# VectorE, not GpSimd, makes the low parts of the weight slabs by default

## Time and profile before

| | us |
|---|---|
| median of three runs | 2493.86 |
| time of the profiled execution | 2493.3 |
| its span, first to last instruction | 2491.5 |
| TensorE busy | 2474.3 |
| VectorE / ScalarE / GpSimd busy | 1116.7 / 1036.4 / 1133.0 |

### The profile page before, as it was taken

How to read it: one execution, slowest core, us unless ns; L and a number is a source line. 1 busy time by engine, 2 the same in 40 slices (tenths; PEclk the granted TensorE clock), 3 DMA queues, 4 the chain that set the end, 5 groups by cost and what they waited for, 6 DMA issues and landing times.

```text
span 2491.5 us, 32310 instructions
## 1 busy us (share of the span) xinstructions
PE 2474.3 (99%) x12882; PEld 2119.1 (85%) x12882; DVE 1116.7 (45%) x2339; ACT 1036.4 (42%) x2012; POOL 1133.0 (45%) x651
## 2 busy tenths in 40 slices
PE   9999999999999999999999999999999999999998
PEld 8888898888889888889888888888898888888887
DVE  7682486755415632325144545423232446434313
ACT  7552487742335322235343333333343443333323
POOL 3354355544445554444434445444544435444442
PEclk9999999999999999999999999999999999999999
DMA  5233332245332553322322222223322222222232
GB/s 213 76 102 103 94 84 75 64 161 192 138 128 85 191 198 112 104 93 77 118 76 85 85 81 88 86 86 100 110 93 85 85 77 81 89 89 81 93 97 81
DMA packets 89237, 258.79 MB, mean 104 GB/s; under 512 B 8961, under 2 KB 30209, under 8 KB 88705
## 3 DMA queue, kind: packets, MB, share of 16 engines
q1 hardware_dynamic: 89088, 256.74, 30.8%
HBM read 246.22 MB, written 2.10 MB: 100 GB/s over the span
## 4 chain that ended last, share of the span: by engine, by line
PE 91%; DVE 4%; ACT 3%; issue 1%; POOL 0%; DMA 0%; DVEq 0%; SPq 0%; POOLq 0%; ACTq 0%
PE bank L1829 89%; PE bank L1839 2%; ACT PP L2047 1%; DVE pt_lo L2350 0%; DVE Y L2350 0%; DVE nt L2350 0%; DVE C L2350 0%; DVE PP L2609 0%; ACT pt_hi L2047 0%; ACT Hhi L2047 0%; ACT blkv L2047 0%; ACT blkk L2047 0%; ACT w_hi L2047 0%; DMA XR<-in_x 0%; POOL n L2915 0%
## 5 line engine op out<-in xcount | busy, mean ns | idle before, releaser
L2910 POOL TENSOR_TENSOR w_lo<-w_raw,w_hi 128x1024 fp32r<-128x1024 f32 (+1 forms) x302 | 747.3, 2477 | 877.6 <-ACT w_hi L2047 877.4
L1829 PE MATMUL bank<-Hhi,w_hi 128*128 128x512 f32 (+1 forms) x1636 | 634.1, 388 | 0.0
L1829 PE MATMUL bank<-Hlo,w_hi 128*128 128x512 f32 (+1 forms) x1636 | 626.9, 383 | 0.1
L1829 PE MATMUL bank<-Hhi,w_lo 128*128 128x512 f32 (+1 forms) x1636 | 626.8, 383 | 0.0
L2047 ACT ACTIVATE w_hi<-w_raw 128x1024 fp32r<-128x1024 f32 (+1 forms) x318 | 326.2, 1030 | 139.2 <-DMA w_raw<-in_wa 82.5
L1829 PEld LDWEIGHTS bank<-Hhi,w_lo 128*128 128x128 f32 x1636 | 307.7, 188 | 61.5
L1829 PEld LDWEIGHTS bank<-Hlo,w_hi 128*128 128x128 f32 x1636 | 308.5, 189 | 53.4 <-POOL w_lo L2910 0.5
L1829 PEld LDWEIGHTS bank<-Hhi,w_hi 128*128 128x128 f32 x1636 | 308.2, 188 | 52.8
L2910 POOL TENSOR_TENSOR w_fifth_lo<-w_fifth_raw,w_fifth_hi 128x1024 fp32r<-128x1024 f32 x77 | 189.9, 2467 | 216.3 <-ACT w_fifth_hi L2047 216.3
L1829 PE MATMUL bank<-Hhi,w_fifth_hi 128*128 128x512 f32 x404 | 159.6, 395 | 0.0
L1829 PE MATMUL bank<-Hhi,w_fifth_lo 128*128 128x512 f32 x404 | 157.8, 390 | 0.0
(11 more groups left out here) (411 smaller groups left out, 4687.6 us busy)
## 6 DMA issues: line engine op xcount, KB each, us to landing
w_raw<-in_wb SPq DMA_DIRECT2D x169, 512.0 KB, 3.3
w_raw<-in_wa SPq DMA_DIRECT2D x139, 512.0 KB, 3.4
wm<-in_w_ada SPq DMA_DIRECT2D x48, 512.0 KB, 4.5
w_fifth_raw<-in_wb SPq DMA_DIRECT2D x42, 512.0 KB, 3.3
w_fifth_raw<-in_wa SPq DMA_DIRECT2D x35, 512.0 KB, 3.4
QQ<-Y SPq DMA_DIRECT2D x64, 128.0 KB, 2.4
wa_raw<-in_wb SPq DMA_DIRECT2D x5, 512.0 KB, 6.1
XR<-in_x SPq DMA_DIRECT2D x4, 512.0 KB, 7.6
```

The costliest lines, as they stand in the source:

```text
L1829: return self.e.matmul(o, lhs, rhs, start=start, stop=stop)
L2910: self.e.tensor_tensor(x.lo[:, k:k + n, :], x.raw[:, k:k + n, :], f(x.hi[:, k:k + n, :]), ALU.subtract).then_inc(*w_rest(s, k))
```

## The change

The default engine of cut_to changes from "pool" to "dve". Calls that name an engine are as before, and so are the order of the walk, the slots, the DMAs and the roundings.

```
-        def cut_to(self, s, n=8, by="pool"):
+        def cut_to(self, s, n=8, by="dve"):
             while self.cut <= s and self.cut < self.sent:
                 for k in range(0, 8, n):
                     self.round_weights(self.cut, self.slot[self.cut], k, n)
                     self.rest_weights(self.cut, self.slot[self.cut], k, n, by)
                 self.parts[self.cut], self.rested[self.cut] = n, dve_rest if by == "dve" else w_rest
```

## The result

The changed kernel takes 2542.39 us (median of 4 runs, 2538.97 to 2544.28) against 2493.89 for the kernel before (2493.67 to 2494.07): a ratio of 1.0192, 95% interval 1.018 to 1.0205. It is 48.5 us slower. The forecast was 2500.2, its range ended at 2509. The profiled execution took 2541.4 us with a span of 2539.6, 48.1 more than the span before.

The account below looks back on a forecast made before the run. TensorE was taken as the bound, busy 2474.3 of 2491.5 us. Terms 2.6 + 4.3 + 0.3 - 0.9 = +6.3 on the profiled 2493.3 gave 2499.6, with the median 0.6 above: 2500.2 us; range 2494 to 2509.

Parts of the forecast that it names:

- The NSA stage: 300 to 505 us: 14 rests add 17.1 us to VectorE, partly covered by waits for pt_hi; a quarter charged, +4.3.
- all in series: Upper bound for the NSA stage: all 17.1 us of added rests delay the kernel, +17.
- Plain products and recurrence: Rests queued 16 us ahead of use, so nobody waits; recurrence and modulations included, +0.3, bounds 0 and +3.
- The start: Three rests ahead of the second half's norm in VectorE's gapless queue delay Ek, the reciprocal and ht: +2.6, bounds 1.2 and 4.5.
- the blocking rule: VectorE and GpSimd share a port pair, the later blocked for an instruction; without GpSimd's rest, Hlo gets 0.6 us back.
- Small gains: TensorE's waits for Y's product and for a GpSimd rest at 826 us shrink by 0.5 and 0.4: -0.9.
- (b): VectorE bounds the NSA stage: rests cost up to 1.9 us, 14 times, about half hidden; +13 there, 2509; chance 0.09.
- (c): Late rests: VectorE's recurrence backlog outgrows the 16 us lead and TensorE waits for w_lo; 2505; chance 0.02.
- (a): Hidden after all: returned blocking shortens the start's delay and NSA waits for pt_hi take the rests; 2495; chance 0.37.
- (d): A gain: waits ended by VectorE or GpSimd shrink and no new one comes; 2488; chance 0.04.
- (e): The change does not do what it says: true only for four half slabs staying on GpSimd, at no cost.
- TensorE's idle time from 300 to 510 us: Sign that the forecast is right: TensorE's idle time there rises from 3 to some 7 us.

Follow-up runs that it names:

- late_nsa: Changed kernel with only the whole-slab rests of the NSA stage (slabs 50 to 63) queued one slab later on VectorE; 2522.27 us, ratio 1.0112.
- wait_only: Kernel before, GpSimd still making all rests, VectorE only waiting at each whole rest's place for ScalarE's rounding; 2518.94 us, ratio 1.0102.
- work_only: Kernel before, GpSimd still making all rests, VectorE doing an unused sum of about a rest's length at each place, without waiting for ScalarE; 2517.99 us.
- nsa_only: Kernel before with VectorE making only the 14 rests of slabs 50 to 63, those of the NSA stage; 2516.65 us, ratio 1.0092.
- wait_work: Kernel before, GpSimd still making all rests, VectorE waiting for ScalarE's rounding and then doing an unused sum at each place; 2547.89 us, ratio 1.0218.
- hold_short: Kernel before with TensorE held up 14 times between retention projection products, each for 4 GpSimd settings of spare columns; 2508.05 us, ratio 1.0058.
- hold_long: Kernel before with TensorE held up 14 times between retention projection products, each for 22 GpSimd settings of spare columns; 2568.97 us, ratio 1.0303.

## Why the prediction was wrong

**The NSA stage, +4.3 forecast, +27.0 measured: the step that failed.** It took the 14 rests as work of 17.1 us, gave it VectorE's 24.6 us of waits for pt_hi as cover, and charged a quarter. Three things were wrong. (1) The waits belonged to the item. GpSimd waited 877 and 216 us ahead of its rests, and the prediction read those rows for durations only; on VectorE the waits stand in the queue of pt_lo and small. late_nsa shows the size: with most of them gone, the same work costs 4.9, close to the 4.3. The old queue shows that there is a wait, and not how long it will be: in this stage GpSimd, held up ahead of its scalings too (25.4 us), waited only 5.8 and 2.1 us ahead of rests, where VectorE waited 17.1 and 4.2. (2) The upper bound, "all in series", was the work's and not the work's and the waits': 17.1 of work and 17.1 + 4.2 us of waits for w_hi and w_fifth_hi, as measured on VectorE, would have held it; with GpSimd's 7.9 us of waits it would have come to 25.0, still under the 27.0. (3) The stalls bring the clock down, 13.7 us at 1.2 GHz in this stage, some 6 us by the estimate above; the prediction had no such term, though stalls of several us were part of two of its rivals. Cover existed all the same. The row of the changed kernel (300 to 505 us) that answers to the earlier trace rows:
```profile
DVE pt_lo L2350 <- ACT pt_hi L2047: 10.4, 14, 2.2
```
More than half of the 24.6 us of waits went, and the stage still lost 27: idle time was no cover, because a rest took VectorE at the time ScalarE set and not in the gap.

**Plain products and recurrence, +0.3 forecast, bounds 0 and 3; +16.7 measured between 80 and 300 us.** The sentence that failed is "Queued behind it is the taking of the next product's result from PSUM, which TensorE finishes one slab later, so nobody waits". True from 517 us on. In recurrence, groups and gmlp VectorE has KS, kc and wst behind the rest, and the recurrence's own XC and TI, which ScalarE waits for in turn. The stalls are few and long: lost time of 3.6 us on KS at 123, 3.4 on w_lo at 181, 3.2 on wst at 258, each with 3.4 us at 1.2 GHz behind it. Here wait_only loses 12.4 and work_only 4.4. The prediction added up VectorE's work over 100 us and found it under 100; an average says nothing on what one item holds up.

**The start, +2.6 forecast, +2.2 at the first products of H, +3.2 at 80 us: right.** This execution was 0.4 us early ahead of the first rest; counted from there it is +2.7 and +3.6. VectorE's timeline in the changed kernel, to be read beside the earlier trace rows:
```profile
22.34 1.22 DVE L2350 TENSOR_TENSOR w_lo<-w_raw,w_hi 128x1024 fp32r<-128x1024 f32 x1
23.48 2.41 DVE L2350 TENSOR_TENSOR Ek<-bank,RT 64x128 f32<-64x128 f32 x8
25.92 1.23 DVE L2350 TENSOR_TENSOR w_lo<-w_raw,w_hi 128x1024 fp32r<-128x1024 f32 x1
27.07 0.16 DVE L2393 RECIPROCAL rstds<-rstds 128x2 f32<-128x2 f32 x1
...
28.22 0.42 DVE L2350 TENSOR_TENSOR Hlo<-ht,Hhi 128x256 fp32r<-128x256 f32 x1
...
35.31 1.23 DVE L2350 TENSOR_TENSOR w_lo<-w_raw,w_hi 128x1024 fp32r<-128x1024 f32 x1
36.57 0.87 DVE L2358 SCALAR_TENSOR_TENSOR ht<-XR,par,bank 128x256 f32<-128x256 f32 x2
```
Each step is where it was put: the rests ahead of Ek, behind Ek and ahead of ht, Hlo at 0.42 instead of 1.04, as the blocking rule had it. Ek is 0.7 late and not 1.2, the reciprocal 1.6 and not 2.2, ht 2.2 and not 2.8: the first rest began 0.5 earlier than assumed, 0.4 of it because all of this execution was early, and the rest of the chain follows. A full queue without waits is where counting work is the right method.

**Small gains, -0.9 forecast; -1.4 from 517 to 830 us: right.** The two that were named are there, -0.65 at Y's product (658 us) and -0.35 at 826; a third, -0.43 at 767, was not named. They were spent again: +1.7 between the layers (1825 us, TensorE waits 1.2 us for nB) and 0.9 in small steps.

**The rivals.** (b), at 0.09, had the right stage and named the wait for the rounding. It priced a rest at up to 1.9 us, half of it hidden; measured, a rest cost 1.6 us in nsa_only (22.0 / 14) and 1.9 in the changed kernel (27.0 / 14), with nothing hidden. The blocking that it named was small: six rests between 300 and 565 us took 1.3 to 1.6, 1.4 us over 1.22 in all, each beside a GpSimd instruction. VectorE did not become the bound by load. The range's upper end, 2509, was said to hold two thirds of (b)'s loss, but (b) with half of it already gives 2509; two thirds of the 27 would have been some 2514, which would not have held the result either. (c) happened once, at 181 us, behind 11 us of scans on VectorE, and with the clock behind it (5.2 us) is a tenth of the loss. (a) and (d) needed a full cover in the NSA stage and are refuted. (e) held as stated. Of what was to show it, the length of the rests and GpSimd's 199 us came as written, TensorE took its first product of Hlo at 38.1 (38.7 forecast), TensorE's idle time from 300 to 510 us is 19.2 and not some 7, and the part behind the NSA stage ended 1.2 us later and not within 1; the list had nothing on the stretch from 80 to 300 us.

What stays open: how much of the changed kernel's start and end is returned blocking (only argued from wait_work), and why the waits and the work together cost 5.5 us more than their sum in the NSA stage (21.2 against 15.7 was measured). No run tried a rounding earlier in ScalarE's queue, which would shorten the waits without moving the rests.

## What to carry to other kernels

When an instruction moves to another engine's queue, its wait moves with it: look for idle time in front of it in the old queue as a sign that it waits, work out from the engine that it waits for how long the new queue, which may come to it earlier, will stand there, and ask for each thing behind it who waits. Spare time on the new engine is cover only if the item is ready before the gap begins. And bound a stall of TensorE by its length and what the clock takes behind it, which in this kernel was about a quarter of the whole loss, by the estimate above.

## What the hardware did that was not expected

The clock. In the kernel before the granted clock is at 2.4 GHz from the first product to the last. In the changed kernel it fell to 1.2 GHz seven times, 3.4 us long six times and 6.8 once, in the last us of a stall of TensorE (496.8) or up to 1.4 us behind one: at 25.7 us (1.5 us idle for Ek, then eight one-column products), 128.1, 186.2, 261.3, 336.3, 442.2 and 496.8. The length of one stall does not decide it alone. In nsa_only TensorE idled 3.31 us and the clock stayed up:
```profile
476.44 0.66 PE L1840 MATMUL bank<-ident,PP 128*128 128x128 f32 x4 [3.31 <-DVE pt_lo L2351]
```
```profile
476.00:480.00 4.00, 3.56 (x24) 3.25 (x25) 3.71 (x12) 2.75 (x8) 0.00 (x0) 1.00 0.01 3
```
and of fourteen stops of 0.86 us in hold_short none brought it down, of fourteen of 3.74 us in hold_long eleven did, while in the changed kernel it fell behind 1.5 us of idle time and eight short products. A second small thing: each short hold cost 1.03 us where TensorE's start-to-start gap lost 0.86; most of the 0.17 more is in the first matmuls behind the hold, which start 0.34 and 0.24 us apart instead of 0.23.
